# Ready-made masks, matmuls of full shape and a small first tile in a two-block layer kernel on one Trainium2 core

## The reference

```python
h = rmsnorm(x, mix_pre_norm)              # sum of squares over 1024 channels
u = h @ w_in                              # u_z, u_xbc, u_dt (16 columns), u_ly, u_lx, u_g
...
# sliding window: 8 query heads of 64, 2 key/value heads of 64
s = jnp.einsum("bnqkgd,bnskd->bnkgqs", q, kb) * (SW_HD ** -0.5)
o = jnp.einsum("bnkgqs,bnskd->bnqkgd", p, vb)
```

## Time and profile before

| | |
|---|---|
| median of 3 runs | 869.72 us (869.59 to 871.77) |
| profiled execution: its own time | 871.67 us |
| its span, from first to last instruction | 869.8 us |
| mean granted TensorE clock over the span | 0.995 of full speed |
| TensorE busy | 848.3 us (98%) |
| VectorE, ScalarE, GpSimd busy | 624.1, 509.0, 78.4 us |
| first matmul | 8.53 us |
| DMA | 149.21 MB, mean 172 GB/s |

### The profile page before, as it was taken

How to read it: one execution, slowest core, us unless ns; L and a number is a source line. 1 busy time by engine, 2 the same in 40 slices (tenths; PEclk the granted TensorE clock), 3 DMA queues, 4 the chain that set the end, 5 groups by cost and what they waited for, 6 DMA issues and landing times.

```text
span 869.8 us, 14548 instructions
## 1 busy us (share of the span) xinstructions
PE 848.3 (98%) x5760; PEld 776.0 (89%) x5760; DVE 624.1 (72%) x1124; ACT 509.0 (59%) x826; POOL 78.4 (9%) x83
## 2 busy tenths in 40 slices
PE   5999999999999999999999999999999999999997
PEld 5999999899989999999998799899899887778885
DVE  6787987988868766666665979777555467775765
ACT  5655778665367755555656787554544445544453
POOL 0200001201020111111112100500000100000000
PEclk9999999999999999999999999999999999999999
DMA  9457443466454655555554463844322243365541
GB/s 342 140 190 286 160 140 119 150 211 256 155 199 150 238 188 194 174 182 202 176 194 169 146 198 124 308 147 146 97 98 97 98 145 122 125 213 191 196 145 49
DMA packets 40588, 149.21 MB, mean 172 GB/s; under 512 B 4524, under 2 KB 4680, under 8 KB 39880
## 3 DMA queue, kind: packets, MB, share of 16 engines
q1 hardware_dynamic: 40520, 148.27, 50.2%
HBM read 147.18 MB, written 1.08 MB: 170 GB/s over the span
## 4 chain that ended last, share of the span: by engine, by line
PE 87%; DVE 7%; ACT 3%; issue 2%; DMA 1%; SPq 0%; DVEq 0%; ACTq 0%
PE bank L610 39%; PE bank L605 16%; PE bank L607 15%; PE bank L606 15%; PE bank L613 2%; DVE t_wl L1741 2%; DVE t_arena L1756 1%; DVE t_arena L1746 1%; ACT t_arena L1235 1%; DVE t_x L1756 1%; ACT t_hh L1235 1%; DMA t_x<-in_xin 1%; ACT t_wh L1230 1%; DVE t_sm L1753 1%; ACT t_br L1235 0%
## 5 line engine op out<-in xcount | busy, mean ns | idle before, releaser
L1741 DVE TENSOR_TENSOR t_wl<-t_raw,t_wh 128x1024 fp32r<-128x1024 f32 x260 | 316.6, 1226 | 112.1 <-ACT t_wh L1230 111.0
L1230 ACT ACTIVATE t_wh<-t_raw 128x1024 fp32r<-128x1024 f32 x260 | 273.4, 1058 | 128.3 <-PE bank L610 60.6
L605 PE MATMUL bank<-t_hh,t_wh 128*128 128x256 f32 x1144 | 330.3, 289 | 2.9 <-DVE t_hl L1746 1.5
L607 PE MATMUL bank<-t_hh,t_wl 128*128 128x256 f32 x1144 | 323.5, 283 | 0.0
L606 PE MATMUL bank<-t_hl,t_wh 128*128 128x256 f32 x1144 | 323.5, 283 | 0.0
L605 PEld LDWEIGHTS bank<-t_hh,t_wh 128*128 128x128 f32 x1144 | 219.1, 192 | 6.8 <-issue 4.2
L606 PEld LDWEIGHTS bank<-t_hl,t_wh 128*128 128x128 f32 x1144 | 219.2, 192 | 0.8
L607 PEld LDWEIGHTS bank<-t_hh,t_wl 128*128 128x128 f32 x1144 | 219.1, 191 | 0.0
L610 PE MATMUL bank<-t_wh,t_br 128*128 128x512 f32 x384 | 123.5, 392 | 0.2 <-POOL t_br L2454 0.2
L1756 DVE SCALAR_TENSOR_TENSOR t_arena<-bank,t_par,t_arena 128x255 f32<-128x255 f32 (+2 forms) x184 | 75.2, 474 | 45.0 <-ACT t_arena L1235 44.7
L610 PE MATMUL bank<-t_wh,t_hh 128*128 128x512 f32 x224 | 91.9, 410 | 1.8 <-DVE t_wl L1741 1.8
(11 more groups left out here) (154 smaller groups left out, 850.3 us busy)
## 6 DMA issues: line engine op xcount, KB each, us to landing
t_raw<-in_ws SPq DMA_DIRECT2D x260, 512.0 KB, 3.9
t_br<-decay SPq DMA_DIRECT2D x1, 2048.0 KB, 8.4
t_arena<-in_post SPq DMA_DIRECT2D x3, 512.0 KB, 4.9
t_arena<-gates SPq DMA_DIRECT2D x1, 1536.0 KB, 10.6
t_x<-in_xin SPq DMA_DIRECT2D x4, 256.0 KB, 5.9
t_bd<-in_bd SPq DMA_DIRECT2D x1, 1024.0 KB, 11.6
t_x<-in_xtok SPq DMA_DIRECT2D x1, 1024.0 KB, 5.8
t_arena<-in_mem SPq DMA_DIRECT2D x1, 1024.0 KB, 8.1
```

Of the source, the lines that this page charges most:

```text
L605: e.matmul(o, wh, xh, start=first, stop=False, skip_group_check=True)
L607: return e.matmul(o, wl, xh, start=False, stop=last, skip_group_check=True)
L1230: e.activation(WH[q % NS][:, :], RAW[q % NR][:, :], ACT.Copy, bias=0.0, scale=1.0).then_inc(*hi.now(q))
L1741: e.tensor_tensor(WL[q % NS][:, :], RAW[q % NR][:, :], WH[q % NS][:, :].bitcast(F), SUB).then_inc(*lo.now(q))
```

## The change

- The chunk dt leaves the stream. Its 16 columns of weights come with the norm's weight in one small tile (`first`, DTW), are split with two small instructions, and go through 16 matmuls with 256 moving columns and 32 or 16 output columns. The low and high sums come in different partitions and are added by a matmul with a constant "fold" in place of the transposes.
- x is loaded in two pieces, before unit 0. The constants come in two parts, and the wide masks and bd come later, between units.
- TensorE first does five float32 matmuls on zeros.
- ScalarE's second split goes between the squares. VectorE adds up to one eighth, so that the sums of this norm, of the memory's and of the SSD's take fewer matmuls; the first norm's are put inside xbc4's second unit, and the spreading inside xbc5's first. 1/rms of the first norm comes from a Sqrt on ScalarE, a reciprocal and one Newton round.
- g0 goes unit by unit. In `h_parts` VectorE splits unit 4 half way.
- pl0 waits for each quarter of its input where it needs it.
- The masks INCL, SAME, INCS and two of 16 x 16 blocks are constants.
- Sliding window: the keys lie in two tiles padded with zeros (SWK2), so that the scores take all 128 partitions; the values' matmuls give all 128 columns.
- FFN: the last low part is made by VectorE, and `sqrt_table` stands behind ScalarE's last high part.

```diff
-    s.append(("dt", "w_in", rng(DTC, 128)))
...
-CON = [("ident", 128), ("ones", 128), ("strict", 128),
-       ("b16", 128), ("b32", 128), ("b64", 128)]
+CON = [("ident", 128), ("ones", 128), ("fold", 16), ("incl", 128), ("up16", 128),
+       ("low16", 128), ("b32", 128), ("b64", 128), ("same", 128), ("incs", 128)]
+NFIRST = 272
...
+            e.dma_start(DTW, first).then_inc(s_first, 16)
+            for i in range(2):
+                e.dma_start(X[:, 4 * i:4 * i + 4, :], xin[:, 4 * i:4 * i + 4, :]).then_inc(s_x[i], 16)
             fetch(0)
+            e.dma_start(conT[:, 0:NFIRST], con[:, 0:NFIRST]).then_inc(s_con, 16)
+            fetch(1)
             e.dma_start(parT[:, :], par).then_inc(s_par, 16)
...
             for q in range(NR, NU):
+                if q == 6:
+                    e.dma_start(conT[:, NFIRST:], con[:, NFIRST:]).then_inc(s_masks, 16)
+                if q == 10:
+                    e.dma_start(MSK, masks[:, 0:384]).then_inc(s_msk, 16)
+                    e.dma_start(maskD[:, :], masks[:, 384:512]).then_inc(s_msk, 16)
+                if q == 12:
+                    e.dma_start(bdT[:, :, :], bd).then_inc(s_bd, 16)
...
+            def mix_sums():
+                e.wait_ge(s_con, 16)
+                e.wait_ge(*d_add.of("mix", 3))
+                column_sums(7, 0, [SC0[:, 0, :]], True, True).then_inc(*p_norm.now("mix", "sum"))
...
+            def mem_sums():
+                e.wait_ge(*d_add.of("mem", 3))
+                column_sums(3, 0, [MEMQ[:, 0, :]], True, True).then_inc(*p_norm.now("mem", "sum"))
...
-                    m = tr(PB[6][:, 16 * hf:16 * hf + 16], dtr[:, 128 * hf:128 * hf + 128])
+                    m = mm(PB[6][:, 16 * hf:16 * hf + 16], dtr[:, 128 * hf:128 * hf + 128], cn("fold", 16)[0:32, :])
...
-                    m = column_sums(3, 2 * g, [SSQ[:, 4 * g + k, :] for k in range(2)], g == 0, g == 1)
+                    m = column_sums(3, 2 * g, [SSQ[:, 4 * g, :]], g == 0, g == 1)
...
-                    r = slice(64 * a_, 64 * a_ + 64)
-                    kt, q = SWK_[r, 0, :], SWQt[r, i, :]
+                    kt, q = SWK2[:, a_, :], SWQt[:, i, :]
...
-                    o = PB[6][r, :]
-                    mm(o[:, 0:T], SWV_[:, 0, r], pt[:, 0:T], True, False)
-                    mm(o[:, 128:T], SWV_[:, 1, r], pt[:, T:384], False, True).then_inc(*p_sw.now("o", i, a_))
+                    mm(PB[6][:, 0:T], SWV_[:, 0, :], pt[:, 0:T], True, False)
+                    mm(PB[6][:, 128:T], SWV_[:, 1, :], pt[:, T:384], False, True).then_inc(*p_sw.now("o", i, a_))
...
-            chunk_by_k("dt", YBh, YBl, x_weighted)
-            e.wait_ge(s_con, 16)
-            norm_sums_first("mix", 7, SC0)
-            norm_sums_last("mix", 7, SC0)
-            chunk("xbc4", YBh, YBl)
-            norm_spread("mix", 7)
-            chunk("xbc5", YBh, YBl)
+            e.wait_ge(*d_const.of("warm"))
+            for _ in range(5):
+                mm(PB[3][:, 0:T], SC1[:, 0, 0:128], SC1[:, 0, :])
+            e.wait_ge(*d_dt.of("w"))
+            for k in range(8):
+                e.wait_ge(*d_xw.of(k))
+                mm(PB[6][0:32, 0:T], DTS[:, k, :], YBh[:, k, :], k == 0, False)
+                m = mm(PB[6][0:16, 0:T], DTS[:, k, 0:16], YBl[:, k, :], False, k == 7)
+            m.then_inc(*p_dt.now("dt"))
+            chunk("xbc4", YBh, YBl, {(1, 4): mix_sums})
+            chunk("xbc5", YBh, YBl, {(0, 4): lambda: norm_spread("mix", 7)})
             for i in range(4):
                 if i == 0:
-                    chunk_by_k("g0", Hh, Hl, normed("mix"))
-                    e.wait_ge(*d_f.of("mix", 7))
+                    chunk_by_units("g0", Hh, Hl, normed("mix"))
+                    e.wait_ge(*d_const.of("row"))
...
-            e.wait_ge(*d_yb.of(3))
+            def hidden(q):
+                return lambda: e.wait_ge(*d_yb.of(q))
+
             for i in range(4):
-                chunk(f"pl{i}", YBh, YBl)
+                chunk(f"pl{i}", YBh, YBl, {(0, 2 * q): hidden(q) for q in range(4)} if i == 0 else ())
...
-            norm_sums_first("mem", 3, MEMQ)
-            norm_sums_last("mem", 3, MEMQ)
+            mem_sums()
...
-                    if j == 23:
-                        sqrt_table()
                     yield from walk.until(T_FU[j] + 2)
                     e.wait_ge(*d_fp.of(j))
...
                     act(YBh[:, j % 8, :], FF[:, j % 2, :], ACT.Copy).then_inc(*a_fh.now(j))
+                    if j == 23:
+                        sqrt_table()
...
+            e.wait_ge(*d_const.of("one"))
+            act(SM[:, 392:393], SM[:, 392:393], ACT.Sqrt)
+            e.wait_ge(s_first, 16)
+            act(DTS[:, :, 0:16], DTX, ACT.Copy).then_inc(*a_dt.now("w"))
+            for k in range(8):
+                if k % 4 == 0:
+                    e.wait_ge(s_x[k // 4], 16)
+                act(YBh[:, k, :], X[:, k, :], ACT.Copy, scale=WMIX[:, k:k + 1]).then_inc(*a_xw.now(k))
             split(0)
...
             for i in range(4):
                 act(SC0[:, 2 * i:2 * i + 2, :], X[:, 2 * i:2 * i + 2, :], ACT.Square).then_inc(*a_sq.now("mix", i))
+                if i == 1:
+                    split(1)
...
-            act(SWK_[:, 0, :], half(BANK["swkv"], 0), ACT.Copy)
+            e.wait_ge(*g_dn.of("pads"))
+            for a in range(2):
+                act(SWK2[64 * a:64 * a + 64, a, :], half(BANK["swkv"], 0)[64 * a:64 * a + 64, :], ACT.Copy)
...
+                yield from walk.until(T_FU[23] + 2)
+                e.wait_ge(*a_fh.of(23))
+                tt(YBl[:, 7, :], FF[:, 1, :], YBh[:, 7, :].bitcast(F), SUB).then_inc(*d_fp.now("low"))
...
-            def block_masks():
...
-            walk.cols("dt", True)
             walk.cols("xbc4")
             walk.cols("xbc5")
             h_low("mix", SC1)
```

More of the change, by code:

```diff
@@ L2284, in dve_program @@
+            e.wait_ge(*d_rs.last())
+            tt(t, o, o, MUL).then_inc(*d_rs.now("mix", "oo"))
+            e.wait_ge(*d_rs.last())
+            tt(t, t, h, MUL).then_inc(*d_rs.now("mix", "t"))
+            e.wait_ge(*d_rs.last())
+            stt(o, t, 1.5, o, ADD, MUL).then_inc(*d_rs.now("mix"))
+            walk.tick()
+            walk.unit(2)
+            walk.tick()
+            walk.unit(1)
+            walk.tick()
+            h_parts("mix", SC1, X, WMIX, 7, {4: 4})
             e.tensor_copy(ROWR, PB[7][:, 0:T]).then_inc(*d_const.now("row"))
-            walk.cols("xbc5")
@@ L2548, in pool_program @@
             walk.tick()
[L2549 to L2551 removed]
+            for i in range(4):
                 walk.cols(f"pl{i}")
```

189 lines of the change are left out of this document (109 added, 80 removed).

## The result

| | before | after |
|---|---|---|
| median on the same chip | 870.55 us (4 runs, 869.59 to 871.77) | 861.29 us (4 runs, 859.10 to 862.41) |
| profiled execution | 871.67 us | 859.10 us |
| its span, mean granted clock | 869.8 us, 0.995 | 857.3 us, 0.998 |

The account below looks back on a forecast made before the run. TensorE, busy 98% of the span, was taken to bound the kernel. Terms −4.5 − 0.7 − 2.1 − 0.3 − 5.6 + 1.5 = −11.7 us took the profiled 871.67 to 860.0, and the median to 858.0 us; range 854.5 to 863.

Parts of the forecast that it names:

- rival (2): Start gives only 2 of its 5.2 us, x's first piece late or h not keeping up: 861.2 us; chance 0.15.
- the prediction's signs of being wrong: Full-shape pairs not taking 0.57 us, xbc4 starting after 12.5 us, or a new wait over 2 us between 36 and 60.
- The start to xbc4: Start of kernel: x lands at about 4.9 us, xbc4 starts at 10.6 instead of 15.07: −4.5 us, bounds −3 and −5.
- Sums of the norm moved into xbc4: First norm's sums go from before xbc4 into its second unit, 4 records in place of 16: +0.4 us.
- The wait for h: TensorE's 1.5 us wait before g0: 0.7 us of it left, −0.8; ends 0 and 1.5.
- The clock: Between xbc4 and g0's end: 1.2 us lost to a clock fall instead of 1.7, −0.5; ends 0 and 1.7.
- Sums of the other norms: SSD's 16 records become 8, mem's 16 become 4: −2.1 us; a late sum costs up to 1.1 us.
- pl0: Its wait for the last quarter of the LRU moves to k = 6, some 2 us later: −0.3 us.
- Full shapes: Sliding-window heads: values save 0.31 and scores 0.39 us per head, eight heads, −5.6 us; bounds 0 and −6.
- Rival (1): Sliding-window heads: full shapes give nothing, shape changes costing no more than narrow matmuls side by side save: 863.6 us; chance 0.07.
- Sqrt table: Behind the last FFN copy the load loses its cover and ScalarE's chain to mk3 starts later: +1.5 us; bounds 0 and +1.8.
- Rival (3): Sqrt load is absorbed by slack in ScalarE's chain, or the clock never falls at the start: 856.4 us; chance 0.16.

Follow-up runs that it names:

- Experiment 5: After with x loaded in four pieces of 262 KB instead of two of 524 KB: 861.95 us, ratio 0.9895.
- Experiment 7: After with the first norm's sums issued before xbc4 instead of within its second unit: 866.02 us, ratio 0.995.
- experiment 3: After without the five matmuls on zeros at the start: 861.17 us, ratio 0.9892.
- experiment 1: After with the Sqrt table moved back ahead of the last FFN copy: 858.67 us, ratio 0.9868.
- experiment 2: After with sliding-window heads at half shape again, tile of zeros still made: 865.97 us, ratio 0.9949.
- experiment 12: After with the sums of the SSD norm and of mem as they were before: 862.16 us, ratio 0.9903.
- experiment 8: After with Sqrt table early, no matmuls on zeros, and the padded tile's memset behind GpSimd's differences: 859.59 us, ratio 0.987.
- experiment 4: Before with only the full-shape sliding-window heads (padded keys, full-width values): 866.10 us, ratio 0.9951.
- experiment 9: After with the Sqrt table early and sixteen matmuls on zeros instead of five: 859.31 us, ratio 0.9877.
- experiment 10: After with the Sqrt table early and the delta rule's output normalised one weight unit earlier: 858.90 us, ratio 0.9874.
- experiment 11: After with Sqrt table early, delta rule's output normalised one unit earlier, and ten matmuls on zeros: 858.35 us, ratio 0.9853.
- experiment 6: After with g0 again by eighths of h over both units instead of unit by unit: 864.29 us, ratio 0.9931.

## Why the prediction was right, and where it was off

The forecast was 858.0 us (854.5 to 863.0) and the median 861.29: faster, within the range, 3.3 us above the number. The number of rival (2), 861.2, is nearly the measured one, but that is chance: this rival lets the start give 2 of its 5.2 us, and it gave 3.7; the other 1.8 us come from elsewhere. None of the prediction's signs of being wrong came: the full-shape pairs take 0.57 us, xbc4 starts at 11.37, and TensorE has no wait over 0.4 us between 36 and 60 us. Point by point:

- **The start to xbc4: right in mechanism, 0.9 us too large (−3.6, not −4.5).** The term that was mis-sized is the landing of x's first piece, 4.9 us in the forecast and 5.79 measured. The error was to let a transfer land soon after the bytes queued up to its end have moved (594 KB, near 4.5 us in after's trace): the last of its 16 parts came 1.3 us later, when nearly both pieces had moved. The landing moves by 1.2 us between executions, so 4.9 was outside what any of them had. Experiment 5 shows the other end of it, unit 0 paying for what is put ahead of it.
- **Sums of the norm moved into xbc4: right, and the price of the alternative was not in the forecast.** Experiment 7 shows that they carry 4.7 us by the medians; 2.5 of what its trace lost is the clock's.
- **The wait for h: right.** 0.7 of it was to remain, a gain of 0.8. It remained as 0.53 and 0.26 us, on the splits behind h, and the gain is 0.9 in the ledger's pair. The row of the ledger is −0.1 and not −0.7 for two other reasons. The sums took 0.4 as forecast, but dt 0.4 instead of 0.2 (0.74 us for its two f32 matmuls and the change of form around them, 0.42 before). And the −0.5 for the clock is missing, because neither trace of the pair lost anything to it.
- **The clock: open within the range given.** I took 1.2 us lost, half a microsecond less than before. Part of this was counted twice: the 1.95 us taken off to get from the profile to the median are nearly what the two falls cost before's stream (2.1), so the median of before had little left to save. In after's profile and in that of experiment 3 xbc4 lost nothing, in those of experiments 1, 2 and 12 the clock was low for 6.8 us from about 8 or 9 us on, in that of experiment 8 until 16.0. Before's fall is no fixed cost either: it is missing in experiment 4, which has the same start. So this term should have been a spread of 0 to 2.2 us (the most that xbc4 lost with this start, in experiment 8), and before's of at least 0 to 1.4.
- **Sums of the other norms: right.** −2.3 by the ledger, −2.2 by experiment 12, forecast −2.1; no trace has a wait for VectorE's additions there.
- **pl0: right,** −0.48 against −0.3.
- **Full shapes: the records were right and the gain was 0.9 us less.** 0.57 us for two matmuls as forecast, 5.7 us saved over eight heads. What failed is the step from the records to the stream: the sum had no wait of what comes next. 0.9 us of waits for VectorE (603 and 734 us in after's trace) took a part back. The rule that changing a tiling mode drains the engine (the Trainium skill, TensorEngine Tiling, Key Properties) is on the side of experiments 2 and 4; the 2x of tiles side by side would have made experiment 2 the faster one. Rival (1) is out.
- **Sqrt table: right,** +1.4 to +1.5. Rival (3), that it is absorbed, is out.
- **Not in the forecast:** +0.7 us near 549 us, a wait for VectorE that the memset of the padded tile brings on, and −0.26 at the convolutions.

The errors add up to what is missing: 0.9 (x) + 0.6 (0.5 for the clock, 0.2 for dt, −0.1 for h) + 0.9 (shapes) + 0.7 (549 us) − 0.2 (pl0) − 0.2 (sums) − 0.3 (convolutions) − 0.3 (the FFN's low part, which the norm's +1.56 did not contain) = 2.1, against 11.7 − 9.5 = 2.2. Of the rest up to 3.3 us, 0.8 is the baseline (before's median was 870.55 beside after, 869.72 in the forecast) and 0.2 the difference between the ledger's 9.5 and the 9.3 of the medians.

The cause of the slower small steps at 543 us is shown in part. Experiment 8 took the memset away from their front, and the steps took 0.5 us less than in experiment 5 with the same start of GpSimd; no run took GpSimd's other operations away. Which steps are slow goes by kind. In eleven of the twelve traces with the memset in front, it meets a TENSOR_SCALAR step, and this one step takes 0.49 to 0.60 us instead of 0.17. In the twelfth, that of after, it meets steps with two tensors as inputs, TENSOR_TENSOR and SCALAR_TENSOR_TENSOR (from 544.15 on), and these keep their 0.17. Steps of these two kinds are slow, 0.38 to 0.50 us, beside GpSimd's TENSOR_TENSOR. The Trainium skill (SBUF — State Buffer, Who interferes with whom) has a rule of this form for the port pair that VectorE and GpSimd share: an instruction of VectorE with two inputs in SBUF contends with one of GpSimd that reads SBUF, "not with one that only writes it", and a memset only writes. The traces agree on this pair; how much of each slow step is waiting for the port is not shown.

## What to carry to other kernels

Price a shortened piece in the stream together with what the engine meets next: of 5.7 us saved in eight heads 0.9 came back as two waits for an engine that had been just in time, and moving one step of VectorE by a unit removed one of them. A function table belongs in front of the wait that covers it, not behind the copy that ends that wait: the same 1.28 us load cost nothing on one side of it and 1.4 us on the other. And before believing a difference of 1 to 3 us, look in each profile at when the first data landed and at the length of the first matmuls: here x's landing moved the start of one and the same kernel by up to 1.2 us, the clock by up to 2.2 and the moment at which GpSimd happens to begin the middle by up to 0.8. The mean granted clock does not tell: it was 0.999 in the profile of experiment 8, which lost 2.2 us to the low clock before the first recorded change, and 0.998 in after's, which lost nothing. A pair of traces with the same clock history from xbc4 on gave a ledger whose rows add up to the distance between their spans, 4.8 us.

## What the runs showed of the hardware

TensorE starts at 1.2 GHz in all these traces. The records of matmuls on zeros show it, 0.43 us each at first and 0.216 later (experiments 9 to 11); the granted clock is recorded only from its first change on, so a window ahead of that reads 1.00 and must not be believed. The first rise came at 5.5 us with five such matmuls (experiment 1), at 6.1 and 6.7 with ten and sixteen, and at 10.4 in the profile of after, which has five as well. With five it also came at 4.1 (experiment 10) and 6.4 (experiment 6). Where it came at 5.5 the clock fell again at 8.9, during the thin dt matmuls; with ten and sixteen it did not fall, but with five and a rise at 6.4 or 10.4 it did not either. VectorE's steps on 128x8, 0.17 us alone, took up to 0.5 us beside GpSimd's f32 operations on 128x128 and up to 0.6 beside its memset, and 18 of them 3.7 to 5.2 us, depending on when GpSimd began and with what. A DMA of 512 KB landed in 16 parts, spread over 0.7 to 1.9 us for the first piece of x.
